# Whole-width chunks for the first two modulations, and the expert gate's spread in the fifth expert turn

## What is computed

```python
m = silu(cvec) @ w_ada + b_ada                     # 6 modulations of 1024 for each of two conditionings
h = rmsnorm(x, g1) * (1 + m[1]) + m[0]
x = x + m[2] * mixer(h)                            # attention, recurrent branch, merge, output projection
h = rmsnorm(x, g2) * (1 + m[4]) + m[3]
x = x + m[5] * (routed_experts(h) + shared_expert(h))   # 64 experts of width 256, top 8
y = rmsnorm(x, final_g)
```

## Time and profile before

| | |
|---|---|
| median of 3 runs | 969.09 us (967.43 to 971.62) |
| the profiled execution | 965.96 us, span 963.7 us |
| PE busy | 883.8 us, 92% of the span |
| DVE, ACT, POOL busy | 413.2, 253.4, 144.0 us |
| TensorE clock granted, mean | 0.977 of full |
| HBM read, written | 287.16 MB, 22.81 MB |

### The profile page before, as it was taken

The page is one execution under the profiler, slowest core; times in us unless marked ns, Lnnn a source line. Parts: engine busy times, 40 slices in busy tenths (PEclk is TensorE's granted clock), DMA queues, the critical chain, the costliest instruction groups (busy, mean ns, idle before and its releaser), DMA issues.

```text
span 963.7 us, 12124 instructions
## 1 busy us (share of the span) xinstructions
PE 883.8 (92%) x4170; PEld 514.4 (53%) x4170; DVE 413.2 (43%) x947; ACT 253.4 (26%) x415; POOL 144.0 (15%) x213
## 2 busy tenths in 40 slices
PE   4799998999999999999997999999999999999973
PEld 2387875899897764543333444444443444444431
DVE  1562483577665554233331332432342334233445
ACT  2537623344423240221211111111111111111111
POOL 7300000000001041122132012012102111111112
PEclk9799999999999999999998999999999999999987
DMA  9974778422227197799999999999999999999832
GB/s 341 343 252 182 293 262 239 109 89 79 98 89 297 64 415 316 243 340 390 404 388 386 421 403 400 410 403 394 423 404 398 404 420 401 402 406 414 340 107 101
DMA packets 85320, 295.65 MB, mean 307 GB/s; under 512 B 17370, under 2 KB 33814, under 8 KB 60320
## 3 DMA queue, kind: packets, MB, share of 16 engines
q1 hardware_dynamic: 64400, 263.21, 68.7%
q0 software_dynamic: 12176, 27.37, 10.0%
q10 hardware_dynamic: 8704, 4.54, 2.1%
HBM read 287.16 MB, written 22.81 MB: 322 GB/s over the span
## 4 chain that ended last, share of the span: by engine, by line
PE 67%; DMA 19%; DVE 5%; issue 3%; ACT 2%; SPq 2%; POOL 1%; ACTq 1%; POOLq 0%; DVEq 0%
PE bank L1466 21%; DMA gu<-in_w_up_e_dram 12%; PE bank L1485 10%; PE bank L1090 7%; PE bank L1092 6%; PE bank L1091 6%; DMA y_dram<-y_sb,slot_row 4%; DMA chunk_raw<-in_w_ada_dram 3%; PE bank L1503 3%; PE bank L1454 3%; PE bank L1118 2%; PE bank L1359 2%; PE bank L1159 1%; PE bank L1192 1%; PE bank L1541 1%
## 5 line engine op out<-in xcount | busy, mean ns | idle before, releaser
L1466 PE MATMUL bank<-gu,x_t 128*64 128x512 f32 (+1 forms) x1024 | 286.4, 601 | 12.8 <-DMA gu<-in_w_up_e_dram 11.0
L1466 PEld LDWEIGHTS bank<-gu,x_t 128*64 128x64 f32 (+1 forms) x1024 | 102.6, 151 | 167.7 <-issue 162.2
L1485 PE MATMUL bank<-dn,a_t 128*64 128x512 f32 (+1 forms) x512 | 145.3, 597 | 4.1 <-ACT shared_sb L1016 3.5
L1985 DVE TENSOR_TENSOR act_sb<-silu_sb,bank 128x256 f32<-128x256 f32 x40 | 16.9, 422 | 229.4 <-ACT silu_sb L1059 229.4
L1059 ACT ACTIVATE silu_sb<-bank 128x256 f32<-128x256 f32 x40 | 15.4, 385 | 330.0 <-PE bank L1466 330.0
L748 POOL DMA_INDIRECT y_dram<-y_sb,slot_row x27 | 45.9, 1701 | 306.5 <-DVE slot_row L1875 260.6
L1485 PEld LDWEIGHTS bank<-dn,a_t 128*64 128x64 f32 (+1 forms) x512 | 48.5, 150 | 74.0 <-issue 67.4
L1090 PE MATMUL bank<-h_hi,chunk_lo 128*128 128x384 f32 x240 | 84.6, 353 | 0.0
L1092 PE MATMUL bank<-h_hi,chunk_hi 128*128 128x384 f32 x240 | 81.1, 338 | 0.0
L1091 PE MATMUL bank<-h_lo,chunk_hi 128*128 128x384 f32 x240 | 81.0, 337 | 0.0
L736 POOL DMA_INDIRECT xg<-h_dram,slot_tok x42 | 44.0, 1047 | 179.8 <-DVE slot_row L1875 155.5
(11 more groups left out here) (345 smaller groups left out, 1072.7 us busy)
## 6 DMA issues: line engine op xcount, KB each, us to landing
gu<-in_w_gate_e_dram SPq DMA_DIRECT2D x64, 1024.0 KB, 15.7
gu<-in_w_up_e_dram SPq DMA_DIRECT2D x64, 1024.0 KB, 20.8
dn<-in_w_down_e_dram SPq DMA_DIRECT2D x64, 1024.0 KB, 26.0
chunk_raw<-in_w_ada_dram SPq DMA_DIRECT2D x24, 1024.0 KB, 8.9
chunk_raw<-in_w_in_dram SPq DMA_DIRECT2D x18, 1024.0 KB, 5.4
chunk_raw<-in_w_out_dram SPq DMA_DIRECT2D x4, 1024.0 KB, 5.0
y_dram<-zeros POOLq DMA_DIRECT2D x1, 3072.0 KB, 17.6
chunk_raw<-in_w_pa_dram SPq DMA_DIRECT2D x2, 1024.0 KB, 5.0
```

Of the source, the lines that this page charges most:

```text
L1466: mm = pe.matmul(bank[2 + u % 2][at_x, :].rearrange("p (g n) -> p g n", g=2), x_t[:, cols], wide[:, :, k, :], start=(k == 0), stop=(k == K ...
L1485: mm = pe.matmul(bank[5 + half][at_x, :], a_t[:, cols], dn[slot_of(x, first)][:, wc], start=(k == 0), stop=(k == 1))
```

## The change

1. The eight chunks of the first two modulations hold two row slices (k = 2c and 2c+1) of all 1024 columns, in rows of 4 KB, where they held four slices of 512 columns. Each chunk still gives four products of 32 columns by 512, now two into bank 6 and two into bank 7, on four different strips. Both halves are finished by the fourth chunk; DVE copies the first half, ACT the second.
2. `spread(1)` and its copies leave the place between merge and output projection, and PE no longer waits there for `bc_evac` 8.
3. POOL copies `m_row[1]` to a tile of its own, `m_late`, once the last input projection is done (the row's old place is overwritten by the second normalisation). `m_late` lies over the second half of `gate_ffn`, so the third copy waits for all four products.
4. PE makes the four products at the end of the first group's turn 4 (the fifth), into banks 3, 0, 1 and 4, behind waits for the copies that free these. ACT copies them at the end of its turn 4. PE's turn 5 waits for the first copy ahead of `gate_up` and for the last ahead of the token transposes.
5. DVE's wait for the gate goes from ahead of the first group to its use (`shared_add`, turns 6 to 8).

```diff
+        m_late = at("m_late", [P, D], 28)
...
+        SPREAD_TURN = 4
+        def spread_bank(n):
+            return bank[(2 + (SPREAD_TURN + 1) % 2, 0, 1, 4)[n]]
... # SP
+                if kind == "ada" and i < 8:
+                    a, c = divmod(i, 4)
+                    sp.dma_start(dst[:, :].rearrange("p (k n) -> p k n", k=2),
+                                 w_ada[0].rearrange("(p k) n -> p k n", k=KD)[:, 2 * c:2 * c + 2, D * MODS[a]:D * MODS[a] + D]).then_inc(loaded, 16)
... # POOL, ahead of its wait for merge_done
+            pool.wait_ge(S["w_mm"], NPROJ)
+            pool.wait_ge(S["row_biased"], 32)
+            pool.tensor_copy(m_late[:, :], m_row[1][:, :]).then_inc(S["late_row"], 1)
... # ACT
+            for a in range(2):
+                act.wait_ge(S["ada_mm"], 4 * a + 4)
+                act.activation(m_row[a % 2][:, 512:1024], bank[7][:, :], ACT.Copy).then_inc(S["ada_row"], 1)
...
-            spread_copy(1, gate_ffn, 1.0)
             split_high(act, number[("out", 1)])
...
+            act.wait_ge(S["late_row"], 1)
             for t in range(TT):
                 act.wait_ge(S["out_done"], TT + t + 1)
... # ACT's block_turn, last in a turn
+                    if first and u == SPREAD_TURN:
+                        spread_copy(1, gate_ffn, 1.0)
... # PE
+            def modulate_first(a):
+                for c in range(4):
+                    n = number[("ada", 4 * a + c)]
+                    pe.wait_ge(chunk_loaded[slot[n]], arrival[n])
+                    if n == 0:
+                        pe.wait_ge(S["cond_silu"], 1)
+                    if c == 0 and a:
+                        pe.wait_ge(S["mod_copied"], a)
+                    for h in range(2):
+                        for j in range(2):
+                            q = 2 * ((c + h) % 2) + j
+                            at_w = j * D + 512 * h
+                            mm = pe.matmul(bank[6 + h][q * QW:(q + 1) * QW, :], cond_t[:, 2 * c + j, :],
+                                           chunk_raw[slot[n]][:, at_w:at_w + 512], start=(c < 2), stop=(c >= 2))
+                    mm.then_inc(S["ada_mm"], 1)
             for a in range(2):
-                for h in range(2):
-                    modulate(a, h)
+                modulate_first(a)
                 turn_rows(a)
...
-            pe.wait_ge(S["merge_gated"], 2 * KD - 4)
-            spread(1)
             pe.wait_ge(S["hl_ready"], 1)
             pe.wait_ge(S["merge_gated"], 2 * KD)
             pe.transpose(bank[6][0:8, 0:P], h_last[:, :], ident[:, :]).then_inc(S["hl_mm"], 1)
-            pe.wait_ge(S["bc_evac"], 8)
             for c in range(4):
... # PE's block_turn
+                    if first and u == SPREAD_TURN + 1:
+                        pe.wait_ge(S["bc_evac"], 5)
                     gate_up(u, b, first)
...
+                    if first and u == SPREAD_TURN + 1:
+                        pe.wait_ge(S["bc_evac"], 8)
                     turn_tokens(i + 1, u + 1, first)
...
                     block_rows(i + 3, u + 3)
+                    if first and u == SPREAD_TURN:
+                        pe.wait_ge(S["late_row"], 1)
+                        pe.wait_ge(S["x_first"], i + 2)
+                        pe.wait_ge(S["x_second"], i + 2)
+                        pe.wait_ge(S["a_ready"], i + 1)
+                        for n in range(4):
+                            spread(n, spread_bank(n), m_late)
... # DVE
             for a in range(2):
-                for h in range(2):
-                    row(a, h)
+                dve.wait_ge(S["ada_mm"], 4 * a + 4)
+                row(a, 0)
                 mod_sum(a)
...
             def shared_add(t):
+                dve.wait_ge(S["bc_evac"], 8)
...
-            dve.wait_ge(S["bc_evac"], 8)
             block_turn(0, True)
```

More of the change, by code:

```diff
@@ L326, in hybrid_step @@
             dve_step pool_turn sp_turn num_step onehot_ready idx_mm idx_ready xgt_mm x_first x_second silu_done act_ready
-            at_mm a_ready y_ready x2_ready y_done out_stored dn_half y_half y_low place_made place_mm place_out""".split()}
+            at_mm a_ready y_ready x2_ready y_done out_stored late_row dn_half y_half y_low place_made place_mm place_out""".split()}
         chunk_loaded = [sem(f"chunk_loaded{i}") for i in range(SLOTS + 2)]
@@ L471, in load_weights @@
                 by_k = dst[:, :].rearrange("p (k n) -> p k n", k=KD)
-                if kind == "ada":
+                if kind == "ada" and i < 8:
+                    a, c = divmod(i, 4)
+                    sp.dma_start(dst[:, :].rearrange("p (k n) -> p k n", k=2),
+                                 w_ada[0].rearrange("(p k) n -> p k n", k=KD)[:, 2 * c:2 * c + 2, D * MODS[a]:D * MODS[a] + D]).then_inc(loaded, 16)
+                elif kind == "ada":
                     a, h, r = i // 4, i // 2 % 2, i % 2
@@ L861, in spread_copy @@
                 for n in range(4):
-                    act.wait_ge(S["bc_mm"], 4 * i + n + 1)
-                    act.activation(dst[:, n // 2, 512 * (n % 2):512 * (n % 2) + 512], bank[(4, 0)[i] + n % 2][:, :],
+                    act.wait_ge(S["bc_mm"], 8 if i and n == 2 else 4 * i + n + 1)
+                    act.activation(dst[:, n // 2, 512 * (n % 2):512 * (n % 2) + 512], (spread_bank(n) if i else bank[4 + n % 2])[:, :],
                                    ACT.Copy, scale=scale).then_inc(S["bc_evac"], 1)
@@ L1126, in turn_rows, with spread @@
                 mm.then_inc(S["m_spread"], 1)
[L1128 to L1135, removed]
+            def spread(n, out, row):
+                pe.matmul(out[:, :], pick[:, n // 2, :], row[:, 512 * (n % 2):512 * (n % 2) + 512],
+                          start=True, stop=True).then_inc(S["bc_mm"], 1)
+            def modulate_first(a):
[13 more added lines that the diff above has]
+                    mm.then_inc(S["ada_mm"], 1)
             for a in range(2):
-                for h in range(2):
-                    modulate(a, h)
+                modulate_first(a)
                 turn_rows(a)
@@ L1224, in _ @@
             modulate(5, 1)
-            spread(0)
+            pe.wait_ge(S["pick_made"], 1)
+            pe.wait_ge(S["row_biased"], 16)
+            for n in range(4):
+                if n >= 2:
+                    pe.wait_ge(S["bc_evac"], n - 1)
+                spread(n, bank[4 + n % 2], m_row[0])
             pe.wait_ge(S["ada_row"], NADA // 2)
```

## The result

The changed kernel takes 959.0 us (median of 8 runs, 957.59 to 959.91). The kernel before has a median of 967.1 us over eight runs, the three that the prediction had among them; the ratio to the runs timed beside the changed kernel is 0.9928 with an interval of 0.9911 to 0.9944. That puts the kernel before at about 966.0 us and the gain at 7.0 us (5.4 to 8.6). The profiled execution takes 959.44 us with a span of 957.6 (before: 965.96 and 963.7), mean granted clock 0.979 (0.977).

A forecast was written before the change was run, and what follows sets the result against it. PE's path was taken to bound the kernel up to about 410 us, the expert weight stream afterwards. Terms -0.8, -4.1 and a hidden +4.1 gave -4.9 us: 961.1 from the profiled execution, written as 964.1 by the median; range 961.5 to 968.0.

The forecast's parts named there:

- the sum: Whole kernel: 0.8 us won by longer rows, 4.1 by moving the spread, its cost in turn 4 hidden: -4.9 us.
- I take zero and keep both for the range: Last modulation chunk: up to 0.9 us won at full clock, about 0.5 lost by a later clock rise; counted as zero.
- The row rate: First modulations' eight chunks: 4 KB rows instead of 2 KB take about 3.9% less time, 0.8 of 21.6 us.
- the third rival: Last modulation chunk: products and transposes run at full clock, 0.9 and up to 1.0 us more won; 962.2 us, chance 0.10.
- The rival that row length doesn't matter: First modulations' chunks: longer rows win nothing, only the spread's move its 4.1 us; 965.0 us, chance 0.18.
- Part 2: Between merge and output projection: without the spread the projection starts 4.1 us sooner, bounds 3.9 and 4.3.
- Part 3: First group's turn 4: the spread makes PE 4.1 to 4.2 us late, hidden by queued weight transfers; nothing reaches the end.
- reserve: DMA queue behind turn 4: 6.4 us of earlier transfers, less a 4.1 us delay, leave 2.3 us of work.
- The paid rival: Expert turns: the queue runs dry behind turn 4, the stream loses up to 4.1 us; 968.3 us, chance 0.14.
- The slower rival: First modulations: products on strips of two banks run one by one, 3.75 us a chunk; 977 us, chance 0.08.

The follow-up runs named there:

- parts 2 to 5 alone: The changed kernel with the first modulations' chunks as in the kernel before: 961.74 us, ratio 0.9955 (0.9932 to 0.9978).
- the run with 2 KB rows: The changed kernel with each of the eight chunks fetched by two DMAs of half its columns: 960.76 us, ratio 0.9949 to the kernel before.
- turn 1 run: The changed kernel with the four spread products in the first group's turn 1 instead of turn 4: 963.52 us, ratio 0.9978 to the kernel before.
- the doubled spread: The changed kernel with the four spread products made twice in turn 4: 961.26 us, ratio 0.9954 to the kernel before.
- neither set alone: The changed kernel plus unused products: twelve in the first modulations, 956.63 us, ratio 0.9937; or two in the second normalisation's waits, 958.77 us, ratio 0.9923.
- both together: The changed kernel with the twelve unused products in the first modulations and the two in the second normalisation: 955.8 us, ratio 0.9890 to the kernel before.
- `cond_t` without `b_t`: The changed kernel with `cond_t` no longer waiting for the load of `b_t`, DVE waiting where it uses it: 959.55 us, ratio 0.9943.

## Why the prediction was right or wrong

The direction and parts 2 and 3 were right; the number was 5.1 us too high, by two steps: 3.1 us are the base, and the other 2.0 are gain that the sum lacks, which the stages place in part 1.

**The base.** The sum was made against the profiled execution, 965.96 us, and then put on the median of three runs, 969.09. The prediction says that the profiled execution lies "inside their spread"; it lies below all three (967.43 to 971.62), which ought to have been a warning that three runs don't settle a median. The five runs of before taken beside the changed kernel have a median of 965.9 us, those beside the experiments 964.8 to 965.7, the largest set, 34 runs, 965.2. Against the 966.0 that the ratio gives, 3.1 of the 5.1 us are this choice, and it is the step that put the result outside the range: set on 966.0, the range would begin at 958.4 and hold 959.0. Put on the profiled execution the forecast is 961.06, 1.62 us above the profiled run of after.

**Part 1, the clock.** The gain is 7.0 us where the sum has 4.9. The term of the sum that failed is "I take zero and keep both for the range". The row rate was right: 393 to 408 GB/s from 16 to 28 us, 3.7% less time for a byte against the 3.9% forecast,

```profile
16.00:28.00 12.00, 8.31 (x68) 2.47 (x66) 2.63 (x6) 0.00 (x0) 4.97 (x9) 1.00 1.06 393
```
```profile
16.00:28.00 12.00, 8.52 (x69) 3.29 (x67) 1.25 (x4) 0.82 (x2) 4.96 (x9) 1.00 1.03 408
```

(before, then after), and the chunk came 1.04 us sooner for 0.8. But the products then gained 0.87 us by the clock, done before it fell, and the projections' start, 1.91 us sooner, became 2.27 by the second projection: the clock also rose again earlier (0.94 granted from 40 to 42 us, 0.50 in before), where the forecast feared that it could not. This is half of the third rival, which had a chance of 0.10 at 962.2: in after the products ran at full clock, the transposes behind them at half (1.97 us). At full clock these take 1.16 us, so they would have given 0.8 us and not the 1.0 of the rival.

What of this reaches the end is less sure. At the second projection the six traces with 4 KB rows and no filler there are 2.3 to 3.9 us ahead of before, not 0.8. By the ratios it is worth 1.3 us alone and 2.6 in the change (against parts 2 to 5 alone), with intervals that don't exclude 0.8. And the trace of parts 2 to 5 alone, 2.5 us behind after at the second projection (50.41), is level with it at the output projection (294.22, in after 294.39): from 166 to 170 us the granted clock is 0.57 in after and 1.00 there. (In before the clock falls at this place too, so before and after can be compared.) One execution can lose by the clock later what another lost by it here.

The rival that row length doesn't matter is refuted by the run with 2 KB rows: its last chunk lands at the old time. The Trainium skill (DMA: Bandwidth & Descriptors, Specifications) has 512 B as enough for line rate; that run against the changed kernel, 29.88 to 28.57 us for the last chunk and 393 to 408 GB/s, doesn't agree, and the measurement decides.

**Part 2.** Forecast: the output projection starts at 297.25 us, with DVE's gated value as releaser. Measured: 294.39, plus the 2.90 us by which the merge came sooner, is 297.29, and the releaser is that value. The second chunk's split came in time, and POOL's copy held up nobody that the chain shows.

**Part 3.** Forecast: a wait of 0.45 and 3.75 us of products, share 0.98 or more behind it, 2.3 us of reserve, PE's wait down from 5.61 to about 1.5. Measured: 0.55 and 3.67, 0.98 to 1.02, 1.7, and 1.72. The reserve was a quarter smaller than forecast and still held. The turn 1 run and the doubled spread show that both halves of the argument carry it: in a stage that isn't full the work is paid, and beyond the reserve it begins to be paid in turn 4 too. The paid rival is refuted for the change as it stands.

**The slower rival** is refuted by the first line of the timeline of after: sixteen products on strips of two banks take 3.64 us (3.67 in one bank). Its time, by its own terms, is 976.4 us or more rather than 977.

## What to carry to other kernels

Work that must be done somewhere costs next to nothing in a turn whose transfer queue is full and holds more than the work's length; read that reserve as time to landing there less time to landing in an idle queue. Where PE waits for transfers and its clock falls behind that, a transfer that comes 1 us sooner can be worth more than that: here 2.3 to 3.9 us at the next stage, of which the times show 1.3 to 2.6 at the end, with wide intervals. Filler products in such a wait are worth a trial but no sure gain: by the ratios neither set alone was clear of the changed kernel's time, and both together were 3 to 4 us under it. Put a forecast on the execution that its terms were read from, and take three runs that all lie on one side of it as a sign that the base isn't known. Before a gain is read from one trace, look for clock falls elsewhere in it that the other trace doesn't have.

## What the runs showed of the hardware

**A small load beside longer rows.** The 24 KB of `b_t`, in pieces of 32 bytes on ACT's queue, land late where SP's queue beside it moves rows of 4 KB; before, then after:

```profile
b_t<-in_b_ada_dram ACTq DMA_DIRECT2D x1, 24.0 KB, 10.3
```
```profile
b_t<-in_b_ada_dram ACTq DMA_DIRECT2D x1, 24.0 KB, 14.4
```

The five traces with 2 KB rows have 10.3 to 10.4 us, the eight with 4 KB rows 14.1 to 14.5. The Trainium skill (DMA: Bandwidth & Descriptors, Queues, rings and completion order) says that each DMA engine takes the queues in turn and drains a whole packet before it goes on to the next; the trace goes that way if longer rows make longer packets beside the small pieces, which no run shows, and the time rose by two fifths, not to twice. Here it cost nothing that the total shows: `cond_t` without `b_t` has the time of the changed kernel within its interval.

**The clock differs between executions of like kernels.** With 4 KB rows and no filler the second projection begins at 46.22 to 47.88 us in six traces, with PE's clock down for some stretch between 30 and 40 us in each; in two of them it had been down ahead of the last chunk too (0.57 granted from 24 to 28 us) and was up again when that came. With fillers the second projection begins at 45.43, with the clock up all this while, and at 46.04, with the clock down from 33 to 36 us. In the second normalisation the clock fell in two traces of thirteen (both with 10.34 us for the routing), in kernels that do there what the others do.
